# The routed experts of a two-block transformer: the next pair's dispatch ahead of the up products, from the sixth pair on, and the last down products by halves

## The reference, cut to what matters

```python
def _hierarchical_moe(h, w_group, w_expert, w_gate, w_up, w_down):
    ...                                   # top group, then top 2 of its 8 experts, for each token
    def expert_block(args):
        xb, e = args
        return (jax.nn.silu(xb @ w_gate[e]) * (xb @ w_up[e])) @ w_down[e]
    ...
    contrib = y[dest] * w_sorted[:, None].astype(y.dtype)
    return jnp.zeros((n, d), y.dtype).at[tok_sorted].add(contrib)
```

## Time and profile before

| | |
|---|---|
| time, median of 3 runs (lowest, highest) | 1016.91 us (1016.75, 1019.25) |
| time of the profiled execution | 1018.49 us |
| its span, first to last instruction | 1016.8 us |
| PE busy | 987.2 us, 97% |
| VectorE, ScalarE, GpSimd busy | 550.7, 344.2, 81.8 us |
| mean granted clock of TensorE, as a share of full | 0.995 |
| HBM read | 310.47 MB |

### The profile page before, as it was taken

The page is one execution under the profiler, slowest core; times in us unless marked ns, Lnnn a source line. Parts: engine busy times, 40 slices in busy tenths (PEclk is TensorE's granted clock), DMA queues, the critical chain, the costliest instruction groups (busy, mean ns, idle before and its releaser), DMA issues.

```text
span 1016.8 us, 15438 instructions
## 1 busy us (share of the span) xinstructions
PE 987.2 (97%) x5970; PEld 688.3 (68%) x5970; DVE 550.7 (54%) x1043; ACT 344.2 (34%) x574; POOL 81.8 (8%) x118
## 2 busy tenths in 40 slices
PE   8899999999999998999999999999999999999997
PEld 6898799999999997889865444444444444443342
DVE  7557689899989998839435422222222222222222
ACT  5555664545445555446341211111111111110112
POOL 7300110111111200200002000000000000000000
PEclk9999999999999999999999999999999999999999
DMA  8334176798879754354747899999999999999993
GB/s 301 125 125 166 66 258 228 275 337 298 310 281 351 285 203 165 131 202 166 305 191 258 329 365 424 414 431 425 428 427 429 429 426 429 427 429 427 429 422 160
DMA packets 60006, 312.15 MB, mean 307 GB/s; under 512 B 4117, under 2 KB 5498, under 8 KB 47418
## 3 DMA queue, kind: packets, MB, share of 16 engines
q1 hardware_dynamic: 52160, 284.83, 70.0%
q0 software_dynamic: 7392, 26.54, 7.3%
q10 hardware_dynamic: 410, 0.16, 0.1%
HBM read 310.47 MB, written 1.05 MB: 306 GB/s over the span
## 4 chain that ended last, share of the span: by engine, by line
PE 86%; DMA 6%; DVE 5%; ACT 2%; issue 1%; POOL 1%; SPq 0%; DVEq 0%; ACTq 0%
PE bank L903 12%; PE bank L904 12%; PE bank L905 12%; PE bank L1423 10%; PE bank L1451 10%; PE bank L1407 9%; PE bank L1351 6%; DMA eslots<-in_w_up 4%; PE bank L1050 3%; PE bank L1368 3%; DMA ring<-in_w_in 2%; PE bank L978 1%; PE bank L1016 1%; DVE ring_r L1871 1%; ACT ring_r L1529 1%
## 5 line engine op out<-in xcount | busy, mean ns | idle before, releaser
L903 PE MATMUL bank<-hT_r,ring_r 128*128 128x256 f32 x664 | 190.0, 286 | 1.1 <-DVE ring_r L1871 1.1
L905 PE MATMUL bank<-hT_r,ring_r 128*128 128x256 f32 x664 | 188.5, 284 | 0.0
L1871 DVE TENSOR_TENSOR ring_r<-ring,ring_r 128x2048 fp32r<-128x2048 f32 (+1 forms) x74 | 164.5, 2258 | 11.4 <-ACT ring_r L1529 11.0
L1529 ACT ACTIVATE ring_r<-ring 128x2048 fp32r<-128x2048 f32 (+1 forms) x74 | 136.6, 1889 | 40.1 <-DMA ring<-in_w_up 34.8
L904 PE MATMUL bank<-v_tok_r,ring_r 128*128 128x256 f32 x496 | 140.5, 283 | 0.0
L903 PEld LDWEIGHTS bank<-hT_r,ring_r 128*128 128x128 f32 x664 | 128.1, 193 | 1.9 <-DVE ring_r L1871 1.3
L905 PEld LDWEIGHTS bank<-hT_r,ring_r 128*128 128x128 f32 x664 | 128.0, 193 | 0.0
L1423 PE MATMUL bank<-eslots,scratch 128*64 128x512 f32 x512 | 114.5, 600 | 5.3 <-issue 3.0
L1451 PE MATMUL bank<-eslots,scratch 128*64 128x512 f32 x496 | 113.4, 596 | 0.7 <-ACT scratch L1761 0.7
L1407 PE MATMUL bank<-eslots,scratch 128*64 128x512 f32 x512 | 112.7, 593 | 0.0
L2352 DVE TENSOR_TENSOR scratch<-scratch,bank 128x512 f32<-128x512 f32 x16 | 11.0, 687 | 158.8 <-PE bank L1423 158.8
(11 more groups left out here) (308 smaller groups left out, 1449.7 us busy)
## 6 DMA issues: line engine op xcount, KB each, us to landing
eslots<-in_w_gate SPq DMA_DIRECT2D x31, 2048.0 KB, 25.7
eslots<-in_w_up SPq DMA_DIRECT2D x30, 2048.0 KB, 20.1
eslots<-in_w_down SPq DMA_DIRECT2D x28, 2048.0 KB, 24.3
ring<-in_w_up SPq DMA_DIRECT2D x16, 2048.0 KB, 11.7
ring<-in_w_in SPq DMA_DIRECT2D x9, 2048.0 KB, 7.9
ring<-in_w_down SPq DMA_DIRECT2D x8, 2048.0 KB, 9.1
kT<-in_w_ada POOLq DMA_DIRECT2D x24, 512.0 KB, 7.7
ring<-in_w_out SPq DMA_DIRECT2D x4, 2048.0 KB, 8.1
```

Source lines behind the costliest of these rows:

```text
L903: pe.matmul(dst, lhs[0], rhs[0], start=start, stop=False, **flags)
L905: return pe.matmul(dst, lhs[1], rhs[0], start=False, stop=stop, **flags)
L1529: sc.activation(hi, raw, ACT.Copy).then_inc(s_whi, 1)
L1871: last = ve.tensor_tensor(lo, raw, hi, ALU.subtract)
```

## The change

From pair 5 to pair 14 dispatch(p + 1) stands between the gate products and the up products of pair p. The rows of pair p are then still being read while those of p + 1 arrive, so the rows rotate through three buffers: `xeT` and two in `used_once`. The waits of dispatch (`s_yV`, `s_oneh`) move with it. VectorE's `tokens(p + 1)` moves ahead of its wait for the up products. VectorE and ScalarE get pairs 0 to 4 as a loop over single pairs, and pairs 5 to 14 as a loop of two turns over five written out. Pairs 0 to 4 and pair 15 keep their order on TensorE, except that the last pair's down products go by halves of rows: both column halves of the first two row blocks, then both of the last two.

```diff
+        later_xeT = [used_once[:, n * KD * P:(n + 1) * KD * P].rearrange("p (k s) -> p k s", k=KD) for n in range(2)]
+        xeT_of = (xeT, later_xeT[0], xeT, later_xeT[0], later_xeT[1])
...
             def pair(p, u, r=None, last_one=False):
+                ahead = r is not None
+                xe = xeT_of[u % PERIOD] if ahead else xeT
...
                     last.then_inc(s_eg, 1)
+                if ahead:
+                    pe.wait_ge(s_yV, 2 * p + 2)
+                    dispatch(p + 1)
                 if not last_one:
                     ready(1)
                 pe.wait_ge(s_combT, p + 1)
...
                 last.then_inc(s_eu, 1)
-                if not last_one:
+                if not last_one and not ahead:
                     pe.wait_ge(s_yV, 2 * p + 2)
                     dispatch(p + 1)
...
-                order = [(f, c) for c in range(2) for f in range(KE)] if last_one else \
-                    [(f, c) for f in range(KE) for c in range(2)]
+                order = [(f + j, c) for f in range(0, KE, KE // 2) for c in range(2) for j in range(KE // 2)] \
+                    if last_one else [(f, c) for f in range(KE) for c in range(2)]
...
             # ScalarE
-            with sc.Fori(0, PAIRS - 1) as p:
+            with sc.Fori(0, PERIOD) as p:
                 pair(p)
+            with sc.Fori(1, PAIRS // PERIOD) as r:
+                for u in range(PERIOD):
+                    pair(PERIOD * r + u, xeT_of[(u + 1) % PERIOD])
...
             # VectorE
                 last.then_inc(s_onehw, 1)
+                if next_xeT is not None:
+                    tokens(p + 1, next_xeT)
                 ve.wait_ge(s_eu, p + 1)
...
-                if not last_one:
+                if not last_one and next_xeT is None:
                     tokens(p + 1)
...
-            with ve.Fori(0, PAIRS - 1) as p:
+            with ve.Fori(0, PERIOD) as p:
                 pair(p)
+            with ve.Fori(1, PAIRS // PERIOD) as r:
+                for u in range(PERIOD):
+                    pair(PERIOD * r + u, xeT_of[(u + 1) % PERIOD])
```

More of the change, by code:

```diff
@@ L220, in two_block_kernel @@
         combT = piece(T, P, of=scratch_r)
+        later_xeT = [used_once[:, n * KD * P:(n + 1) * KD * P].rearrange("p (k s) -> p k s", k=KD) for n in range(2)]
+        xeT_of = (xeT, later_xeT[0], xeT, later_xeT[0], later_xeT[1])
+        assert len(xeT_of) == PERIOD
         ye_sum = scratch[:, off[0] + D:off[0] + 2 * D]
@@ L1406, in pair @@
                     for e in range(2):
-                        last = pe.matmul(GB[64 * e:64 * e + 64, :], xeT[:, k, 64 * e:64 * e + 64], weights(0, e, k),
+                        last = pe.matmul(GB[64 * e:64 * e + 64, :], xe[:, k, 64 * e:64 * e + 64], weights(0, e, k),
                                          start=(k == 0), stop=(k == KD - 1))
@@ L1422, in pair @@
                     for e in range(2):
-                        last = pe.matmul(UB[64 * e:64 * e + 64, :], xeT[:, k, 64 * e:64 * e + 64], weights(1, e, k),
+                        last = pe.matmul(UB[64 * e:64 * e + 64, :], xe[:, k, 64 * e:64 * e + 64], weights(1, e, k),
                                          start=(k == 0), stop=(k == KD - 1))
                 last.then_inc(s_eu, 1)
-                if not last_one:
+                if not last_one and not ahead:
                     pe.wait_ge(s_yV, 2 * p + 2)
@@ L1744, in _, with tokens, pair @@
             sc.preload_act_table(ACT.Silu)
-            def tokens(p):
+            def tokens(p, xe=xeT):
                 sc.wait_ge(s_dispA, p + 1)
                 for k in range(KD // 2):
-                    last = sc.activation(xeT[:, k, :], PS[4][:, k * P:(k + 1) * P], ACT.Identity, scale=1.0,
+                    last = sc.activation(xe[:, k, :], PS[4][:, k * P:(k + 1) * P], ACT.Identity, scale=1.0,
                                          bias=modc[:, 2, k:k + 1])
                 last.then_inc(s_xeA, 1)
-            def pair(p, last_one=False):
+            def pair(p, next_xeT=xeT, last_one=False):
                 sc.wait_ge(s_eg, p + 1)
@@ L1758, in pair @@
                 if not last_one:
-                    tokens(p + 1)
+                    tokens(p + 1, next_xeT)
                 sc.wait_ge(s_etr, p + 2)
@@ L2335, in tokens, with pair @@
                     c = (k - KD // 2) * P
-                    last = ve.tensor_scalar(xeT[:, k, :], PS[5][:, c:c + P], modc[:, 2, k:k + 1], None, ALU.add)
+                    last = ve.tensor_scalar(xe[:, k, :], PS[5][:, c:c + P], modc[:, 2, k:k + 1], None, ALU.add)
                 last.then_inc(s_xeV, 1)
-            def pair(p, last_one=False):
+            def pair(p, next_xeT=None, last_one=False):
                 ve.wait_ge(s_disp, p + 1)
```

## The result

The changed kernel took 1024.88 us (median of 7 runs, 1022.64 to 1026.46), the kernel before 1019.25 us (median of 7 runs, 1016.75 to 1020.18, the three shown before among them). The ratio is **1.0053**, with a 95% interval of 1.0038 to 1.0068: slower by 5.4 us, between 3.9 and 6.9.

The account below looks back on a forecast made before the run. TensorE sets the pace, 27.03 us a pair, until late weights cost 7.33 us from pair 12. Pairs of 28.0 us without waits plus 0.5 us of tail add 3.0 us: 1018.49 becomes 1021.5 us, range 1018.0 to 1024.0.

Parts of the forecast that it names:

- (a): Up products, pairs 12 to 14: dispatch first gives up weights 3.77 us more, taking back up to 7.33 us.
- (b): Between up products and transposes, pairs 5 to 14: VectorE's product loses its cover, 0.97 us a pair, 9.7 us.
- (c): Waits that move with dispatch, ahead of the up products: cost nothing, with 3.3 us of slack in pair 5.
- (d): Weight requests issued later, gate matrices by 3.77 us: cost nothing, since the DMA queue stays full.
- (e): The three row buffers: take room, not time.
- (f): Last down products by halves of rows, at the kernel's end: +0.5 us, bounds 0 and 2.0.
- The sum: Pair 15 starts 2.4 us later without any DMA wait; with the tail the span grows 2.9, say 3.0 us.
- Against the median: Median lay 1.58 us below the profile, put down to pair 14's low clock; changed runs also at 1021.5 us.
- the offset belongs to profiling: Rival: every profiled execution is 1.58 us above the timed runs, so the changed kernel takes 1019.9; chance 0.25.
- The clock in the short waits: Rival: ten short waits lower TensorE's granted clock, 1.9 us each, up to 1040; chance 0.04.
- Loading of code: Rival: VectorE's and ScalarE's jump back from pair 9 to 10 stalls, 18 us once, 1022 to 1040; chance 0.03.
- The faster side: Rival: VectorE's product costs under 0.38 us a pair exposed, or weights stream slower in timed runs; chance 0.08.

Follow-up runs that it names:

- The halved loads: Kernel before, but pairs 4 to 14 load only the first half of the rows of each expert matrix: 0.9929 of the kernel before.
- the buffers-only kernel: Changed kernel with dispatch, tokens and last down products in their old order, keeping the three row buffers and written-out loops: 0.9997 of the kernel before.
- the gate halves: Half-dispatch kernel, plus the last pair's gate matrices loaded and awaited in halves of rows: 0.9977 of the kernel before, median 1017.17 us.

## Why the prediction was right or wrong

**What bounds the kernel** was read rightly: TensorE's pace first, the stream of weights late, 7.33 us of waits with the low clock in them. The halved loads took 7.4 us off the chain.

**(a)** was right in full: no wait is left, and pair 15's gate matrices land at 981.5, 7.4 us before they are due.

**(b) is the step that failed.** It had the right mechanism and was too small. I took 0.97 us a pair from pair 15's sequence; it measured 281.84 / 10 - 27.03 = 1.15. The product and the transposes behind it cost what pair 15 shows (0.70, and 0.66 for 0.44). What I put at nothing is the switch: moving dispatch puts the up products behind 128-column products, 0.17 us a pair, 1.7 in all. It could be read before the run: the down products stand behind transposes and take 7.02, the gate and up products stand behind 64-column products and take 6.87, with 32 equal products in each.

The prediction also named a wrong reason for the same size. Its upper bound, 1.2 us a pair from the sequencer's lead, would have put the pairs 28.2 us apart and the time at 1023.8, and it took "starts 28.2 apart" as its sign. The starts are 28.18 apart, so by that sign alone it would look confirmed. But the bound put the extra behind VectorE's product, and there nothing was added: transposes 0.66, combine 1.85, transposes 0.22, as in pair 15. The extra lies in the up products, 7.04 for 6.87, and appears there without dispatch or product when a lone transpose stands ahead of them.

**(c), (d), (e)** cost nothing, as said: the buffers-only kernel is at 0.9997, no gap stands ahead of dispatch, the DMA share stayed at 1.00 to 1.01 from 600 to 990 us, and the last down weights land 294.4 us behind pair 5, before the change 294.8.

**(f)** was right: 0.41 to 0.49 for 0.5.

**The sum** gave 280.0 us from pair 5 to pair 15 and, with the tail, +2.9 for the span; without the 2.05 us upstream it measured 281.84 and +4.65. The difference is the switch.

**Against the median** is the second step that failed, and only both together put the time outside the range. The profiled execution was to come at 1021.5 and came at 1025.1. The switch alone would have made 1023.3 of it and the 2.05 us upstream alone 1023.6, both inside the range. The prediction held the low clock behind pair 14's wait for the one piece of chance, and a run without it for the typical one. The four profiled executions with the old order and whole weights show otherwise: all four have that low clock, three in pair 14 (8.78, 8.79 and 8.78 us) and one in pair 13. And a piece of chance that it left out lies where the change doesn't touch anything, behind the wait near 394 us, 1.6 us in the profile after. The profile before had been spared it. The base was low too: three runs, two of them near 1016.8, gave 1016.91, and seven gave 1019.25, 2.3 us higher. Why those two runs were fast stays open, as they have no profile here. A base that still moved with the number of runs should have widened the range upwards.

That the forecast's shift over the base, 4.6 us, lies inside the measured 3.9 to 6.9 is partly luck: the sum gave 3.0, outside it, and the other 1.58 came from this argument about the low clock.

**The rivals.** That the offset belongs to profiling is out: with seven runs the profiled 1018.49 no longer lies above the median. The clock in the short waits: it stayed 1.00 in every stretch of the experts' stage after, up to 990 us. Loading of code: no gap. The faster side needed the cover to be superfluous, and it is not: covering the product took 0.80 us off a pair.

## What to carry to other kernels

When work is moved ahead to give a transfer more time, ask what that work was hiding where it stood: here 3.8 us of dispatch hid 0.7 us of VectorE, and ten exposed products with the switches cost more than three late transfers. Moving half of it kept the cover and still gave the weights time, 27.36 us a pair for 28.19; in the times that came to the kernel before (0.9991, interval up to 1.0004), and with the gate halves 0.2% under it. And measure how far the kernel is from the next bound before paying anything: the weights' stream left 2.6 us to gain in the profile and less in another execution, and the change paid 11.6 to take back waits of 7.4.

## What the runs showed of the hardware

- A group of 32 products with 64 columns of weights takes 0.15 to 0.17 us longer when it stands behind products with 128 columns than behind its own kind (7.02 to 7.04 us against 6.87). The four combine products behind up products took 1.13 instead of 0.93, and dispatch in two halves 3.96 instead of 3.77. Transposes behind up products took 0.66 instead of 0.44, but there VectorE's product lies between, so this may be the same cost or that of the wait.
- TensorE waited 2.16 us and then had 1.2 GHz for some microseconds (up products of 8.78 us in pair 14 before), and after a wait of 2.07 us in pair 13 of the same execution it kept the full clock (7.09 us). In another execution, of the kernel before with the new last order, it was the other way round: the low clock fell behind 2.08 us in pair 13, and pair 14's 0.47 us kept the full one. The same wait of 2.6 us in the feed-forward was followed by the low clock in 8 executions of 13. A fall cost 1.4 to 1.7 us.
- After each pair's wait of some 0.8 us for VectorE in the changed kernel the clock stayed full, ten times of ten.
